# A two-block transformer kernel on one core: eight modulation slabs of the last layer moved from TensorE to VectorE, and two waits of attention moved

## The reference, cut to what matters

```python
s_lat = jax.nn.silu(c)
s_ctx = jax.nn.silu(c_ctx)
for l in range(DEPTH_2):                       # two layers
    ml = jnp.split((s_lat @ w_ada[l] + b_ada[l])[:, None, :], 6, axis=-1)
    mc = jnp.split((s_ctx @ w_ada[l] + b_ada[l])[None, None, :], 6, axis=-1)
    hl = _modulate(_rmsnorm(xl, norm_g[l, 0]), ml[0], ml[1])
    hc = _modulate(_rmsnorm(xc, norm_g[l, 0]), mc[0], mc[1])
    yl, yc = _mixer(hl, hc, ...)               # mLSTM, differential attention, Fourier
    xl = xl + ml[2] * yl
    xl = xl + ml[5] * _swiglu(_modulate(_rmsnorm(xl, norm_g[l, 1]), ml[3], ml[4]), ...)
    ...                                        # the same for xc, but not in the last layer
```

## Time and profile before

| | us |
|---|---|
| median of 3 runs | 3191.98 (3186.93 to 3197.32) |
| the profiled execution | 3191.7 |
| its span, first to last instruction | 3189.9 |
| TensorE busy | 3090.8 (97%) |
| VectorE busy | 1456.3 (46%) |
| ScalarE busy | 601.3 (19%) |
| GpSimd busy | 501.8 (16%) |
| mean granted TensorE clock | 0.991 of full |

### The profile page before, as it was taken

How to read it: one execution, slowest core, us unless ns; L and a number is a source line. 1 busy time by engine, 2 the same in 40 slices (tenths; PEclk the granted TensorE clock), 3 DMA queues, 4 the chain that set the end, 5 groups by cost and what they waited for, 6 DMA issues and landing times. The chain is left out here.

```text
span 3189.9 us, 38386 instructions
## 1 busy us (share of the span) xinstructions
PE 3090.8 (97%) x15962; PEld 2313.9 (73%) x15962; DVE 1456.3 (46%) x2239; ACT 601.3 (19%) x1197; POOL 501.8 (16%) x210
## 2 busy tenths in 40 slices
PE   8999999999999999999999999999999999999998
PEld 4458778775448857887588888888888888678543
DVE  6745531446764256225852344233223512712574
ACT  2113221131112012112521112111021211411110
POOL 3420000003331000121012121211211001000332
PEclk9999999999999999999999999999999999999999
DMA  6554532325551211333032232221222233133452
GB/s 223 198 187 159 212 135 91 123 103 209 183 200 57 80 53 53 141 136 119 1 117 108 106 132 106 80 80 72 99 106 80 80 132 115 70 145 115 159 193 97
DMA packets 46030, 387.06 MB, mean 121 GB/s; under 512 B 7840, under 2 KB 22304, under 8 KB 22560
## 3 DMA queue, kind: packets, MB, share of 16 engines
q1 hardware_dynamic: 41360, 379.35, 32.3%
q10 hardware_dynamic: 4496, 5.24, 0.8%
HBM read 370.67 MB, written 1.05 MB: 117 GB/s over the span
## 5 line engine op out<-in xcount | busy, mean ns | idle before, releaser
L961 PE MATMUL bank<-h_T,weights 128*128 128x256 f32 (+1 forms) x3184 | 774.4, 396 | 15.8 <-ACT h_T L2053 4.0
L961 PEld LDWEIGHTS bank<-h_T,weights 128*128 128x128 f32 x3184 | 600.2, 191 | 157.3 <-issue 71.7
L2654 POOL TENSOR_TENSOR weights<-weights 128x1024 f32<-128x1024 f32 (+2 forms) x103 | 248.1, 2408 | 1700.0 <-DMA weights<-wide_slabs_dram 1600.2
L2663 POOL TENSOR_TENSOR factors<-weights 128x1024 f32<-128x1024 f32 (+2 forms) x103 | 255.3, 2479 | 950.9 <-PE bank L961 769.2
L961 PE MATMUL bank<-arena,weights 128*128 128x256 f32 x1784 | 399.0, 383 | 4.4 <-DVE arena L3347 2.5
L961 PEld LDWEIGHTS bank<-arena,weights 128*128 128x128 f32 x1784 | 340.3, 192 | 57.3 <-issue 5.2
L961 PE MATMUL bank<-weights,h_T 128*128 128x256 f32 (+2 forms) x1040 | 339.4, 474 | 3.4 <-DMA weights<-wide_slabs_dram 2.1
L961 PE MATMUL bank<-factors,weights 128*128 128x256 f32 x1432 | 323.7, 379 | 2.2 <-DVE factors L2942 1.6
L961 PE MATMUL bank<-weights,factors 128*128 128x256 f32 (+1 forms) x936 | 303.4, 469 | 2.9 <-DVE weights L2929 1.8
L961 PEld LDWEIGHTS bank<-factors,weights 128*128 128x128 f32 x1432 | 271.8, 190 | 39.8 <-issue 1.9
L961 PEld LDWEIGHTS bank<-weights,h_T 128*128 128x128 f32 x1040 | 197.6, 191 | 128.6 <-issue 103.3
(11 more groups left out here) (349 smaller groups left out, 2594.1 us busy)
## 6 DMA issues: line engine op xcount, KB each, us to landing
weights<-wide_slabs_dram SPq DMA_DIRECT2D x166, 2048.0 KB, 7.8
weights<-down_slabs_dram SPq DMA_DIRECT2D x8, 1408.0 KB, 6.0
merged_T<-arena SPq DMA_DIRECT2D x240, 32.0 KB, 1.8
arena<-arena ACTq DMA_DIRECT2D x16, 256.0 KB, 12.6
weights<-wide_slabs_dram SPq DMA_DIRECT2D x3, 1024.0 KB, 5.1
masks<-second_consts_dram SPq DMA_DIRECT2D x1, 2176.0 KB, 13.3
masks<-second_consts_dram SPq DMA_DIRECT2D x2, 1024.0 KB, 6.9
factors<-x_T_dram SPq DMA_DIRECT2D x1, 1024.0 KB, 4.8
```

The source lines that it names most:

```text
L961: return mm(out, lhsT, rhs, start=start, stop=stop, skip_group_check=True)
L2654: nc.gpsimd.tensor_tensor(b[2], b[2], b[3], ALU.add).then_inc(S["first_sums"], 1)
L2663: nc.gpsimd.tensor_tensor(e, b[2], b[0], ALU.subtract).then_inc(S["first_sums"], 1)
```

## The change

Of the 12 slabs of layer 1's modulation 4 stay on TensorE, in the places 0, 1, 2 and 11. The other 8 leave the ring. Their weights are stored transposed (outputs on partitions, 1024 inputs along the row), in 32 tiles of 128 x 1024, and VectorE multiplies each tile with the two condition rows and sums along the row in one instruction (`scalar_tensor_tensor` with `accum_out`), 64 instructions in all. They stand in 16 windows of 4 instructions: one in each of the 11 up units (as `inside`, behind the C11 join), and five in the down units. The condition rows are loaded as rows (1 MB) and ScalarE takes their Silu once, 128 x 2048. SP loads two tiles of 512 KB for each window, into two buffers of their own. `layer_prep(1)` moves from behind `down[0]` to behind `down[2]`. Apart from that, ScalarE's copy of unit n-2 in attention now stands between the two exponentials of unit n, in both layers; and the tiny matmuls of dilated attention wait for a new signal, `dil_bank_free`, which VectorE gives once it has read banks 4 to 7, while `dve_for_pe` is waited for ahead of `rwkv_proj0`.

```diff
+ADA1_PLACES = (0, 1, 2, 11)
+ADA_BY_DVE = 12 - len(ADA1_PLACES)
...
+        ADA_PRODUCT = A[:, 14848:15872]
+        COND_ROWS = A[:, 18432:20480]
+        ADA_TILES_AT = {("l0_ffn_up", 0): 0, **{("l0_ffn_up", n + 2): n for n in range(1, 9)}, **{("l0_ffn_down", n): 9 + n for n in range(7)}}
...
+                def ada_tiles(w):
+
+                    if w == 0:
+                        sp.wait_ge(S["dve_out"], ST["l0_fn_proj1"].dve_end)
+                        sp.dma_start(COND_ROWS, par_in[:, NPAR:NPAR + 2 * D]).then_inc(S["cond_rows"], 16)
+                    for b in range(2):
+                        slab, c = divmod(2 * w + b, 4)
+                        if w:
+                            sp.wait_ge(S["ada_vec"], 2 * (w - 1) + b + 1)
+                        src = wide_in[bass.ds(N_WIDE + slab, 1)].rearrange("a p n -> (a p) n")[:, c * 1024:(c + 1) * 1024]
+                        sp.dma_start(ada_tile(b), src).then_inc(S[f"ada_tile{b}"], 16)
                 def load(j, i, st=st):
+                    if (st.name, j) in ADA_TILES_AT:
+                        ada_tiles(ADA_TILES_AT[st.name, j])
...
@@ tensor, dilated attention
             t.wait("act_for_pe")
-            t.wait("dve_for_pe")
+            t.wait("dil_bank_free")
             for q in range(2):
...
             yw = slot3(sR)
+            t.wait("dve_for_pe")
             project(ST["rwkv_proj0"], lambda k: yw[:, k], T, drains=by_dve, frees=act_frees("dil_v", 2))
...
@@ tensor, layer 0 (and so on for the places 4 to 10)
-                        (k0, "P1"): modulate(2, 3),
-                        (v0, "P1"): modulate(3, 4),
-                        (v1, "P1"): modulate(4, None),
+                        (k0, "P1"): modulate(2, None),
...
@@ scalar, attention
                         t.wait("weights_out")
-                        for m in range(2):
-                            ins = af(DA_P(n, m)[:, 0:w], ...)
-                        t.out(ins, "probs_in")
+                        exp(n, 0, w)
                     if n >= 2:
                         k = n - 2
...
                         t.out(af(DA_PT(k)[:, 0:w], bank[2][:, 0:w], ACT.Copy), "pt_ready")
+                    if n < n_units:
+                        exp(n, 1, 512 if DA_ORDER[qtiles][n % qtiles] < 2 else 256)
...
                     shifts(H2, (0, 1), 1, la)
+                    act.wait_ge(S["cond_rows"], 16)
+                    t.out(af(COND_ROWS, COND_ROWS, ACT.Silu), "cond_rows_ready")
...
@@ vector
             for b in range(4):
                 t.wait("pe_for_dve")
                 t.out(ts(part(sV, b), bank[4 + b][:, :], 1.0 / 64, GN_EPS, mul, add), "dve_for_act")
+            say("dil_bank_free")
...
+                    def ada_window(w):
+                        if w == 0:
+                            t.wait("cond_rows_ready")
+                        for b in range(2):
+                            n = 2 * w + b
+                            dve.wait_ge(S[f"ada_tile{b}"], 16 * (w + 1))
+                            for s in range(2):
+                                column = 8 * (24 - ADA_BY_DVE) + 2 * n + s
+                                ins = stt(ADA_PRODUCT, ada_tile(b), 1.0, COND_ROWS[:, s * D:(s + 1) * D], mul, mul, accum_out=ada_all[:, column:column + 1])
+                                if s == 0:
+                                    t.step(ins)
+                            ins.then_inc(S["ada_vec"], 1)
+                            dve.wait_ge(S["ada_vec"], n + 1)
...
                     for j, key in enumerate(up):
-                        unit(key, corner=(lambda: hidden_lat(j - 1)) if j else None)
+                        unit(key, corner=(lambda: hidden_lat(j - 1)) if j else None, inside=lambda: ada_window(j))
                         hidden_ctx(j)
...
                     for j, key in enumerate(down):
-                        unit(key, take=down_added, corner=...)
-                        if j == 0:
+                        unit(key, take=down_added, corner=...,
+                             inside=(lambda: ada_window(len(up) + 2 * j)) if j < 3 else None)
+                        if j < 2:
+                            ada_window(len(up) + 2 * j + 1)
+                        elif j == 2:
+                            vec = ada_all[:, 8 * (24 - ADA_BY_DVE):192].rearrange("p (c s) -> p c s", s=2)
+                            t.step(tt(vec, vec, bc(pc("b_ada", 4 * (24 - ADA_BY_DVE), 4 * ADA_BY_DVE), 2, 2), add))
                             layer_prep(1)
```

More of the change, by code:

```diff
@@ L76, in stage_list @@
     add("mix_out", 2, 0, 0, 0)
-    ada1 = [0]
+    places = [0]
     def modulation(la=0):
         if la == 0:
-            add(f"ada1_{ada1[0]}", 1, 1, 0, 0)
-            ada1[0] += 1
+            if places[0] in ADA1_PLACES:
+                add(f"ada1_{ADA1_PLACES.index(places[0])}", 1, 1, 0, 0)
+            places[0] += 1
     ffn("ffn2")
@@ L909, in _ @@
             sp.dma_start(com[:, :], const_in).then_inc(S["loads"], 16)
-            sp.dma_start(par[:, :], par_in).then_inc(S["loads"], 16)
+            sp.dma_start(par[:, :], par_in[:, 0:NPAR]).then_inc(S["loads"], 16)
             for n, st in enumerate(ORDER):
@@ L2199, in units_out, with gates_free @@
                         after[key]()
-            def gates_free(name, row):
+            def gates_free(name, row=None):
                 def run():
-                    ada_row1(row)
+                    if row is not None:
+                        ada_row1(row)
                     act.wait_ge(S["dve_out"], ST[name].dve0 - 1)
@@ L2537, in _, with exp @@
                 n_units = 8 * qtiles
+                def exp(n, m, w):
+                    sc = stat[:, 4 * (n % 3):4 * (n % 3) + 4]
+                    ins = af(DA_P(n, m)[:, 0:w], bank[4 * m + n % 2][:, 0:w], ACT.Exp, scale=0.125, bias=sc[:, m:m + 1],
+                             accum_out=sc[:, 2 + m:3 + m])
+                    if m == 0:
+                        t.step(ins)
+                    else:
+                        t.out(ins, "probs_in")
                 for n in range(n_units + 2):
@@ L3717, in _ @@
                     for j, key in enumerate(down):
-                        unit(key, take=down_added, corner=(lambda: down_added(down[j - 1], "C21")) if j else lambda: factor_sum(p + "hid", 3))
-                        if j == 0:
+                        unit(key, take=down_added, corner=(lambda: down_added(down[j - 1], "C21")) if j else lambda: factor_sum(p + "hid", 3),
+                             inside=(lambda: ada_window(len(up) + 2 * j)) if j < 3 else None)
[4 more added lines that the diff above has]
+                            t.step(tt(vec, vec, bc(pc("b_ada", 4 * (24 - ADA_BY_DVE), 4 * ADA_BY_DVE), 2, 2), add))
                             layer_prep(1)
@@ L3941, in layout @@
         ffn(g["w_ffn_in_2"][la], g["w_ffn_out_2"][la], la == 0)
-    par = np.zeros((P, NPAR), f)
+    for n in range(12 - ADA_BY_DVE, 12):
+        put(np.concatenate([g["w_ada_2"][1][:, 512 * n + P * c:512 * n + P * (c + 1)].T for c in range(4)], axis=1))
+    par = np.zeros((P, NPAR + 2 * D), f)
+    par[:, NPAR:NPAR + D] = g["c_2"][0].reshape(1, D)
+    par[:, NPAR + D:] = g["c_ctx_2"].reshape(1, D)
     def column(name, v):
@@ L3972, in layout @@
         par[:, n0:n0 + 128] = g["w_in_2"][la][:, 4096:4112].reshape(KT, P, 16).transpose(1, 0, 2).reshape(P, 128)
-    assert len(wide) == N_WIDE and len(down) == N_DOWN, (len(wide), N_WIDE, len(down), N_DOWN)
+    assert len(wide) == N_WIDE + ADA_BY_DVE and len(down) == N_DOWN, (len(wide), N_WIDE, len(down), N_DOWN)
     xT = g["x"][0].reshape(2, P, D).transpose(1, 0, 2)
```

53 lines of the change are left out of this document (17 added, 36 removed).

## The result

| | before | after |
|---|---|---|
| median | 3189.45 us (3185.54 to 3197.32, 4 runs) | 3154.34 us (3151.65 to 3161.03, 4 runs) |
| the profiled execution, its span | 3191.7, 3189.9 us | 3161.03, 3159.1 us |
| mean granted clock, profiled execution | 0.991 | 0.990 |

The ratio is 0.9888 [0.9867, 0.9908]: 35.1 us shorter by the medians, 30.8 us by the two profiled spans (the profiled execution of after is the slowest of its four). Four later runs of the same kernel gave 3160.43 us (ratio 0.9898 [0.9882, 0.9915]); the median of all eight is 3158.1 us, inside it. So on which side of the lower end the median fell was a matter of which four runs were taken.

The account below looks back on a forecast made before the run. TensorE, busy 3090.8 of 3189.9 us, was taken as the bound; 14.8 + 3.7 + 4.2 + 6.9 - 0.2 = 29.4 us shorter, so a median of 3162.5 us, range 3155 to 3176.

Parts of the forecast that it names:

- The slabs: Layer 1's modulation on TensorE: eight slabs' rows go, 14.8 us, and seven sets of transposes, 3.7 us.
- The ring and GpSimd's sums: Weight slabs load no later, and GpSimd's sums S1 and S2 move behind P6: 0, within 2 us either side.
- The multiplies: VectorE in layer 0's feed-forward: 1.4 us each (1.3 to 2.3), a window of four 5.7 us, hidden.
- the budget of 13.6 us: Up units: time VectorE has from the C11 join's end until the C22 join must start for P4.
- Rival (a): Multiplies run at the scan's rate, windows of 9.3 us exceed the budget; 3170 to 3176 us, chance 0.13.
- The first window: First up unit: with GpSimd's pair of sums the window needs 10.4 us against a budget of 10.2, costing 0.2.
- Rival (c): VectorE bounds the up units; gain gone at a 16.3 us window, 3250 us at multiplies of 4.2; chance 0.03.
- What comes with them: ScalarE's Silu (1.91 us), SP's 33 DMAs and small operations stay hidden; the snapshot ends 1.0 us before P6.
- Attention: ScalarE's copy between the exponentials removes TensorE waits: 5.1 + 1.0 us in layer 0, 0.8 in layer 1, 6.9 together.
- Rival (b): The attention edit gives nothing, the copy waiting in ScalarE's queue holds the second exponential; 3169.5 us, chance 0.12.
- The moved wait: First block's dilated attention: tiny matmuls no longer wait for VectorE's L3273, TensorE's 4.24 us idle goes, gain 4.2 us.
- The range: Whole kernel: 3155 to 3176 us, down by 3 us of drain waits and 5 us scatter, up to rival (a).

Follow-up runs that it names:

- the kernel with three multiplies: The changed kernel with each of the 64 multiplies issued three times, the same result written again: 3264.31 us, ratio 1.0229 to before.

## Where the prediction was right, and which term was mis-sized

**The slabs** (14.8 + 3.7 = 18.5 us forecast, 19.4 measured). Rows and columns counted right, and the eighth set of transposes is worth nothing, as worked out. What is missing is 0.1 us for each block that goes: the group of records behind one takes 3.72 us, behind another product 3.62.

**The ring and GpSimd's sums** (0 within 2 us): right. They moved the start of layer 0's attention by 0.8 us, to the good: the sum that had held up L3585 there no longer meets it.

**The multiplies** (1.4 us each forecast, 1.23 + 0.08 measured; hidden: measured 0.00 in the up units). Right, and the budget of 13.6 us that decided it was tested from the other side: at a window of 14.2 us a unit gets 0.83 us longer. Rival (a) is out, the scan's rate was the wrong neighbour and the row of the same operation the right one. The Trainium skill, "Vector Engine (DVE) Microarchitecture Reference", section "Points that are easy to get wrong", says that this form halves its throughput with two SBUF sources that aren't bf16; the rows of L3709 contradict it: 1.23 us for 1024 columns with the sum, just what L2952's `tensor_tensor` takes for 1024 without one. Rival (c) is out too: that point lies at a window of 16.3 us, and the window is 5.1. But the kernel with three multiplies, 19.4 us long, is slower than before, as its mechanism has it; there each microsecond over costs 1.4, not 1.

**The first window** (0.2 us lost forecast, 0 measured): the meeting with the sums that it foresaw took place, two multiplies at 3.25 us. The Trainium skill, "SBUF — State Buffer", section "Who interferes with whom", says that a VectorE instruction with two SBUF inputs contends with a GpSimd instruction that reads SBUF, through a shared port pair that is an exclusive lock. The trace agrees: a multiply of 1.23 us behind a sum of 2.35 us can take up to 3.6, and it took 3.25, and the sum that came behind a running multiply took 3.33 for 2.35. The prediction had priced the meeting at both sums in full, 4.7 us; two multiplies grew by 4.0.

**What comes with them** (0 forecast): right. ScalarE's Silu took 1.92 us (1.91 forecast), and the snapshot behind it ended at 1908.02, 1.0 us before P6, as reckoned.

**Attention** (6.9 us forecast, 8.3 measured with the 0.8 that came with the moved sums; the edit alone 7.6). The wait in a pair is gone, and with it again the 0.1 us behind a wait: 0.47 us a pair, not 0.34. VectorE didn't become late. Rival (b) is out, by the run with this edit alone.

**The moved wait** (4.2 us forecast, 7.4 measured on average). This is the term that was mis-sized. The step said "Gain 4.2 us": it took the wait's length for its price. The row behind it, 9.66 us for 48 tiny records, was on record and I read it as fixed. It is 5.4 to 8.1 us where TensorE doesn't idle ahead of it, and filling that idle time with useless matmuls shortened it to 6.58 without moving the wait. So the idle time drew the clock down, and the step had left out what that cost. The same reading stood in the margin of `rwkv_proj0`, taken as 9.66 us: it is 5.3 to 7.9 us, and no wait stands there in after, so it did no harm.

**The range.** Its lower end allowed for scatter of 5 us and for drain waits in attention, but not for the terms above, which are all too small on the same side: by 0.9, 1.4 and 3.2 us. They make 35 us of 29.4. The rest is the scatter: the eight runs of after lie between 3151.7 and 3161.5 us with a granted clock of 0.993 to 0.990, and before's 48 runs in the four later comparisons have medians of 3189.4, 3191.0, 3193.6 and 3196.8 us at 0.992, 0.991, 0.990 and 0.989. Where the half-clock stretches fall in one execution is not settled by these runs: the same instructions had both levels.

## What to carry to other kernels

Before work is given to a half idle engine, read its budget at one place: from the last thing it did to the first thing that somebody waits for behind the new work, with the neighbour that shares its port laid on top. Here that number, 13.6 us, said within 1 us where 64, 128 and 192 multiplies stop being free, while the busy share (48, 52, 53%) said nothing.

The price of a stall of TensorE is more than its length: 0.1 us for the group that follows, and where the stall is long or stands beside tiny matmuls, the time at half clock behind it, which took the gain of the moved wait from 4.2 to 7.4 us and added almost half to the cost of the waits of 5.6 us. And when a gain hangs on it, put the scatter of the clock into the lower end of the range as well as into the upper.

## What the runs showed of the hardware that was not expected

- A `scalar_tensor_tensor` over two 128 x 1024 float32 tiles in SBUF with its sum along the row takes 1.23 us, and 0.08 us more to read the sum, a record of its own; without a sum, a `tensor_tensor` of that size (L2952) takes 1.23 us too.
- After waits of 5.6 us, 16 records took 5.35 to 6.65 us instead of 3.62. After 4.24 us of idle time, 48 records of 2 columns took 9.7 to 10.4 us, without it 5.4 to 8.1.
- Ten matmuls whose result nobody uses, put into 4.24 us of idle time, made the kernel 4.1 us shorter [1.3, 6.7], and the stretch around them 3.3 us in its trace.
- A VectorE multiply and a GpSimd sum that meet take turns: 3.25 us for 1.23 and 4.06 beside a wider sum, and 3.07 and 3.33 us for a sum of 2.35 that comes while a multiply runs.
- One and the same group of instructions in the norm ahead of the feed-forward ran at full clock in eight traces and partly at half in five, 28.2 against 29.9 to 31.5 us.
